# Expert weights loaded in one contiguous 16 KB run per partition, with both contractions permuted to match

## The reference, cut to what matters

```python
h = rms_norm(x, norm_ffn_w[l])                 # (256, 2048)
...
for e in range(N_EXPERTS):                     # 32
    he = jax.nn.silu(xt @ w1[e]) * (xt @ w3[e])            # w1, w3: (2048, 512)
    y = y + combine[:, e:e + 1] * (he @ w2[e])             # w2: (512, 2048)
```

## Time and profile before

| | |
|---|---|
| runs | 1729.54, 1732.15, 1735.81 us; median 1732.15 |
| span of the profiled execution, first to last instruction | 1727.7 us (the page gives no other time for it) |
| PE busy | 1534.4 us, 89% |
| DVE, ACT, POOL busy | 665.6, 393.2, 211.8 us |
| bytes read and written | 480.9 MB, mean 278 GB/s |
| mixture, from its first gather | 696.9 to 1717 us |
| weight pieces | 192 transfers of 2048 KB, median 18.1 us (19.2 us into `mixT`) from issue to landing |

### The profile page before, as it was taken

How to read it: one execution, slowest core, us unless ns; L and a number is a source line. 1 busy time by engine, 2 the same in 40 slices (tenths; PEclk the granted TensorE clock), 3 DMA queues, 4 the chain that set the end, 5 groups by cost and what they waited for, 6 DMA issues and landing times.

```text
span 1727.7 us, 21935 instructions
## 1 busy us (share of the span) xinstructions
PE 1534.4 (89%) x8398; PEld 939.2 (54%) x8398; DVE 665.6 (39%) x1144; ACT 393.2 (23%) x735; POOL 211.8 (12%) x152
## 2 busy tenths in 40 slices
PE   5888988988986986889999999989989999999996
PEld 4787878888885765443443444344344344344342
DVE  6866677667666354102202212212221221221223
ACT  5435435434434243000111011011011001001002
POOL 2233224224223243000000000000000000000000
PEclk9999999999998998899999999999999999999999
DMA  7543334334342348499999999999999999999994
GB/s 213 130 101 97 101 100 100 97 100 100 97 154 100 98 155 307 154 402 396 395 403 395 397 401 395 399 399 395 402 396 395 403 395 398 400 395 400 398 395 175
DMA packets 268459, 480.88 MB, mean 278 GB/s; under 512 B 11081, under 2 KB 111634, under 8 KB 251026
## 3 DMA queue, kind: packets, MB, share of 16 engines
q1 hardware_dynamic: 268434, 480.54, 77.3%
HBM read 478.43 MB, written 2.10 MB: 278 GB/s over the span
## 4 chain that ended last, share of the span: by engine, by line
PE 61%; DVE 16%; DMA 9%; ACT 6%; issue 5%; SPq 2%; DVEq 0%; ACTq 0%
PE bank L519 60%; DMA ew<-in_expert_w_dram 9%; DVE w_parts L1151 2%; SPq L488 2%; PE bank L522 2%; ACT w_parts L881 1%; DVE ew L1190 1%; DVE misc L1283 1%; DVE misc L1282 1%; ACT ew L1077 1%; DVE ye L1252 1%; DVE ye L1183 1%; DVE ye L1190 1%; DVE ew L1527 1%; ACT hT L1072 1%
## 5 line engine op out<-in xcount | busy, mean ns | idle before, releaser
L519 PE MATMUL bank<-ew,hT 128*64 128x512 f32 (+1 forms) x1600 | 461.4, 581 | 18.5 <-ACT hT L1072 14.0
L519 PE MATMUL bank<-act_parts,w_parts 128*128 128x256 f32 x2304 | 333.8, 298 | 22.2 <-DVE w_parts L1151 17.4
L519 PEld LDWEIGHTS bank<-ew,hT 128*64 128x64 f32 (+1 forms) x1600 | 158.9, 137 | 294.4 <-issue 290.5
L519 PEld LDWEIGHTS bank<-act_parts,w_parts 128*128 128x128 f32 x2304 | 299.1, 198 | 35.3 <-DVE w_parts L1151 19.2
L519 PE MATMUL bank<-ew 128*64 128x512 f32 (+1 forms) x1056 | 240.8, 600 | 21.9 <-DVE ew L1529 19.8
L519 PE MATMUL bank<-mixT,hT 128*64 128x512 f32 x512 | 225.8, 594 | 0.0
L1527 DVE SCALAR_TENSOR_TENSOR ew<-ew,bank 128x256 f32<-128x256 f32 x32 | 13.5, 421 | 515.3 <-ACT ew L1079 515.3
L1594 POOL TENSOR_TENSOR w_parts<-fw,w_parts 128x768 fp32r<-128x768 f32 x64 | 136.6, 2142 | 337.5 <-ACT w_parts L881 337.3
L519 PEld LDWEIGHTS bank<-ew 128*64 128x64 f32 (+1 forms) x1056 | 84.6, 140 | 163.8 <-issue 158.1
L519 PE MATMUL bank<-ye,ew 128*128 128x512 f32 x256 | 122.8, 612 | 15.2 <-DVE fw L1515 13.7
L881 ACT ACTIVATE w_parts<-fw 128x1024 fp32r<-128x1024 f32 x128 | 128.4, 1051 | 16.7 <-PE bank L519 16.4
(11 more groups left out here) (221 smaller groups left out, 1078.2 us busy)
## 6 DMA issues: line engine op xcount, KB each, us to landing
ew<-in_expert_w_dram SPq DMA_DIRECT2D x160, 2048.0 KB, 18.1
mixT<-in_expert_w_dram SPq DMA_DIRECT2D x32, 2048.0 KB, 19.2
fw<-in_w_in_dram SPq DMA_DIRECT2D x48, 1024.0 KB, 5.9
fw<-in_w_out_dram SPq DMA_DIRECT2D x16, 1024.0 KB, 5.1
mixT<-in_x_dram SPq DMA_DIRECT2D x1, 2048.0 KB, 7.6
fw<-in_x_dram SPq DMA_DIRECT2D x1, 2048.0 KB, 10.0
out_dram<-fw SPq DMA_DIRECT2D x2, 1024.0 KB, 3.9
ye<-in_norm_ffn_w_dram SPq DMA_DIRECT2D x1, 1024.0 KB, 4.7
```

The costliest lines, as they stand in the source:

```text
L519: return nc.tensor.matmul(o, l, r, start=start, stop=stop, skip_group_check=True)
```

## The change

`load_expert` takes the weights' rows in another order. Before, partition p of chunk k held row `c*1024 + k*128 + p` of w1 and w3, so that a partition's 8 rows of 2 KB came from 8 places. Now it holds row `16*p + 8*c + k`: 8 rows that stand next to each other, 16 KB in one run. For w2 the two rows of 8 KB of a piece, which came from two places, are now rows `4*p + 2*c + k`, again one run of 16 KB. Size, number, buffers and order of the transfers are as before. To match, `hn` is written in the order k, p (ACT reads `x2` with a step of 16 elements, POOL reads the norm's weights with the same step; what they write is contiguous), and the transposes read `hs` with a step of 4 elements. The router's own transposes and products, and everything behind the mixture, are untouched.

```diff
             def load_expert(e, piece):
                 half, which = piece // 2, piece % 2
                 if piece < 4:
-                    src = (expert_w1, expert_w3)[which][0, e].rearrange("(c k p) n -> p c k n", p=P, c=2)[:, half]
-                    dst = ewp[piece].rearrange("p (k n) -> p k n", n=FF)
+                    src = (expert_w1, expert_w3)[which][0, e].rearrange("(p c k) n -> p c (k n)", p=P, c=2)[:, half]
                 else:
-                    src = expert_w2[0, e].rearrange("(c k p) n -> p c k n", p=P, c=2)[:, which]
-                    dst = ewp[piece].rearrange("p (k n) -> p k n", n=D)
-                sp.dma_start(dst, src).then_inc(s_ew[piece], 16)
+                    src = expert_w2[0, e].rearrange("(p c k) n -> p c (k n)", p=P, c=2)[:, which]
+                sp.dma_start(ewp[piece], src).then_inc(s_ew[piece], 16)
@@
                     for k in range(FC):
-                        l = tr(bank[3][:, k * P:(k + 1) * P], hs[:, k * P:(k + 1) * P])
+                        l = tr(bank[3][:, k * P:(k + 1) * P], hs.rearrange("p (f k) -> p k f", k=FC)[:, k])
@@
             for t in range(NT):
-                act.activation(hn[:, t], x2[:, t], ACT.Copy, scale=stat[:, 4 + t:5 + t]).then_inc(s_hscaled, 1)
+                act.activation(hn[:, t].rearrange("q (k p) -> q k p", k=KD), x2[:, t].rearrange("q (p k) -> q k p", k=KD),
+                               ACT.Copy, scale=stat[:, 4 + t:5 + t]).then_inc(s_hscaled, 1)
@@
                 pool.wait_ge(s_hscaled, t + 1)
-                G.tensor_tensor(hn[:, t], hn[:, t], wffn, ALU.mult).then_inc(s_hn, 1)
+                h3 = hn[:, t].rearrange("q (k p) -> q k p", k=KD)
+                G.tensor_tensor(h3, h3, wffn.rearrange("q (p k) -> q k p", k=KD), ALU.mult).then_inc(s_hn, 1)
```

## The result

| | before | changed |
|---|---|---|
| median | 1731.06 us (20 runs, 1727.88 to 1736.64) | 1734.67 us (20 runs, 1732.16 to 1739.24) |
| ratio | | 1.0019, 95% interval 1.001 to 1.0028 |
| span of the profiled execution | 1727.7 us | 1732.1 us |
| waits of PE for weight pieces | 4.4 us | none |
| mean granted clock of the profiled execution | 0.967 | 0.961 |

What follows compares the result with a forecast made beforehand. Weight transfers (63.2 us a pair) and PE (62.78 us) lay within 1%. Transfers -5.0, transposes 0, `hn` +2.4 made -2.6 us on the 1727.7 us span, 1725.1; with 4.5 us to the median, about 1729.5 us, range 1722 to 1746.

Steps and rivals of the forecast that it cites:

- the falls of the clock: Gather in 3 of 16 pairs: lower granted clock cost 1.7 us each time; the sum left this unchanged.
- the upper end: Whole kernel: 1746 us, for slower strided reads on PE with one or two more falls of the clock.
- The 4.5 us that the forecast put between span and median: Whole kernel: median of the runs, 1732.15 us, above the profiled span of 1727.7 us; added to the predicted span.
- The rate: Weight transfers: 16 KB runs move at 428 GB/s instead of 387 and 422; gain 5.0 us in all.
- Making `hn`: Router: POOL's strided reads lengthen its two instructions, which block DVE, by 2.4 us; ACT taken at 0, at most 2 us.
- the other estimate of 3.4: Router: POOL's cost from the skill page's figure and a 1.2 GHz clock, 1.7 us for each of two instructions.
- The transposes of `hs`: 128 transposes on PE's path, stationary operand read with a 16 B step: taken at 0, upper bound 14.1 us.
- the rival of slower reads: PE's 128 transposes cost 0.11 us more each, 14.1 us in all, giving 1743.6 us; chance 0.25.
- a rival as luck: Gathers: no falls of the granted clock and no POOL cost, -10.8 us, giving 1721.5 us; chance 0.11.
- The gain of the transfers: Mixture: 0.47 us in each of 7 pairs, 3.3 us, plus 1.7 us in the first pair; together 5.0 us.
- 1.7 was taken: First pair: the awaited weight piece lands in 16.5 instead of 18.22 us, taking 1.7 us off a 2.35 us wait.

Runs made afterwards that it cites:

- before_filled_gap: The kernel before, plus one matmul of constants where PE waits for `gT` of each pair's second expert: 1729.93 us, ratio 0.9993.
- hs_only: The kernel before with only the transposes' operand `hs` read with a step of 4 elements: 1730.43 us, ratio 0.9997.
- after_filled_gap: The changed kernel, plus one matmul of constants where PE waits for `gT` of each pair's second expert: 1725.51 us, ratio 0.9963.
- the same edit of PE's order: Next pair's gather issued before the second expert's w2 product: 1729.95 us on the kernel before, 1689.66 us on the changed kernel.

## Why the prediction was wrong

The forecast was 1729.5 us, a gain of 2.6 us; measured was a loss of 3.6 us, inside the range and inside what the text called no change, but on the other side of zero. Two steps failed: the price of 0 for the transposes, which was 3.0 us and alone takes the gain away, and the falls of the clock, kept as a fixed cost, which made it a loss. That the time still lies in the range owes much to its width: the upper end was made for transposes at 14.1 us. The 4.5 us that the forecast put between span and median also mixes two things, 1.8 us between a run's time and its own span (1729.54 and 1727.7) and the spread of three runs; the ratio doesn't depend on it.

- *The rate.* 428 GB/s expected, 432 measured; PE no longer waits for a piece, the DMA share falls under 1.00. Right.
- *Making `hn`.* DVE stands still while POOL works: right, and 2.7 us came against 2.4. POOL's share is 2.1 us, below the 2.4 taken and the other estimate of 3.4. ACT nearly doubled; the remaining 0.6 us came with POOL's later start, where 0 was taken.
- *The transposes of `hs`.* Taken at 0, with 14.1 us as the other end. They cost 3.0 us, so this term of the sum was wrong by that much; the rival of slower reads was right in kind, at about a fifth of its price. The reason given for 0, that the load shares the pace with the 128 columns that follow, doesn't hold: eight transposes, four of them strided, take 1.19 us instead of 1.09. The Trainium skill ("SBUF — State Buffer", Door 1: The DMA port swizzle) was right that an access to a new line each time pays, and its other reading, that a stride of 4 fp32 values is free, is not borne out. The measured price is 69 ns on a load of 140 ns, of which 24 ns reach the path.
- *The falls of the clock.* This is the step of the mechanism that failed. The prediction kept their number and price as they were and put a change of them into a rival as luck. They are coupled with the rest. Before, the pair had a floor at 63.25 us, under which both a fall's 1.7 us and slower transposes disappeared for the most part: before_filled_gap gains 1.4 us, hs_only loses none. The changed kernel has no such floor and pays each in full: after_filled_gap gains 9 us. The 3.6 us of loss are then -4.4 us (both kernels with the gap filled, transposes and router included) plus 9.2 for the changed kernel's falls, less 1.1 to 1.4 for those of before.
- The gain of the transfers was in turn counted too low: with no falls every pair, not 7, ran at the transfers' pace. From 63.25 to 62.75 us in 15 pairs are 7.5 us, where 3.3 was taken. In the first pair, from the first gather to the second w2 product, before_filled_gap took 53.92 us and after_filled_gap 51.90, 2.2 us less when the strided transposes are left out, where 1.7 was taken. With 3.0 for the transposes and 2.7 for the router that makes -4.0 us, near the -4.4 measured.

A profile is one execution; the means of the granted clock over all runs say the same. They are 0.9623 in the changed kernel (20 runs) and 0.9684 with its gap filled (5 runs). With two levels, one half of the other, that is 131 and 109 us at the lower level (an estimate from the clock and the span): 22 us less, some 6 falls of 3.4 us, 11 us of time at 1.7 us each, where 9.2 was won. In the kernel before the same filler takes the mean from 0.9664 (17 runs) to 0.969 (12 runs), 9 us less at the lower level, between 2 and 3 falls or 4.6 us of time, where only 1.4 was won. That is the difference between paying and being covered.

Whether falls are also more frequent at PE's own pace is less sure. The mean is 0.9656 before (35 runs), 0.967 with the slower transposes alone, and 0.9641 with the new loads alone, which fits; but it is 0.9644 with the new `hn` alone, which keeps the transfers' pace and has a longer low stretch over the router, so the mean doesn't count falls of the mixture only. In the profiles no pair at the transfers' pace has a fall except the one that ends that pace. Why 63.25 us would be kinder than 62.78 or 62.94 was not tried apart from filling the gap; it stays open.

## What to carry to other kernels

Where two engines are within 1% of each other's pace, a change that speeds one up should be priced against the floor it removes and against everything that the wait had covered: slower instructions and clock falls that were free are paid afterwards. Before judging a faster load, shorten the other side in both versions and measure again; here the same edit of PE's order brought 0.6 us on the old layout and 45 us on the new one. A permutation for a contraction isn't free on the operand that has to follow it: a step of 16 B cost a weight load half as much again, and one of 64 B cost DVE's instruction over half as much again and ACT's nearly twice.

## What the runs showed of the hardware

- A step of 64 B nearly doubled ACT's 128x2048 float32 instruction (2.0 to 3.75 us each). A DVE instruction of that size took about 3.7 us with the step, another one 2.35 us without. POOL's took 23% longer with one of two operands strided (4.49 to 5.5 us). A step of 16 B took a weight load in a transpose from 140 to 209 ns.
- Small DVE instructions (a TENSOR_TENSOR on one element per partition, usually 0.16 us, and a CAST, usually 0.17 us) stood still for 5.16 and 5.15 us beside a POOL tensor_tensor; others ran beside it at their usual length (MATCH_VALUE_LOAD and FIND_INDEX8, MAX8).
- One otherwise useless matmul of 1.02 us in each gap of 1.15 us, which left 0.32 us of the wait, kept the granted clock up in the mixture from 760 to 1700 us and made the changed kernel 9 us faster.
- A fall of the granted clock to 0.50 lasted 3.4 us and cost 1.7 us; each one in the mixture began within 0.6 us of the first product behind PE's wait for `gT`.
